# A two-layer transformer kernel in float32: the keys' root rows of the second mixer spread over 128 partitions by a DMA from SBUF to SBUF instead of a product with a row of ones

## The reference, cut to what matters

```python
def mla_mixer(z, cos, sin, qa_g, kva_g, w_uq, w_ukv, qn_g, kn_g):
    cq, ckv, kpe = jnp.split(z, [MLA_Q_LORA, MLA_Q_LORA + MLA_KV_LORA], axis=-1)
    q = (rms_norm(cq, qa_g) @ w_uq).reshape(B, S, MLA_HEADS, MLA_QK)
    kv = (rms_norm(ckv, kva_g) @ w_ukv).reshape(B, S, MLA_HEADS, MLA_NOPE + MLA_VDIM)
    k_nope, v = kv[..., :MLA_NOPE], kv[..., MLA_NOPE:]
    k_rope = jnp.broadcast_to(kpe[:, :, None, :], (B, S, MLA_HEADS, MLA_ROPE))
    k = jnp.concatenate([k_nope, k_rope], axis=-1)
    q = rms_norm(q, qn_g)
    k = rms_norm(k, kn_g)
    q = jnp.concatenate([q[..., :MLA_NOPE], apply_rope(q[..., MLA_NOPE:], cos, sin)], axis=-1)
    k = jnp.concatenate([k[..., :MLA_NOPE], apply_rope(k[..., MLA_NOPE:], cos, sin)], axis=-1)
    o = causal_block_attention(q, k, v)
    return o.reshape(B, S, MLA_HEADS * MLA_VDIM)
```

## Time and profile before

| | us |
|---|---|
| median of 3 runs | 1857.9 (1856.42 to 1859.65) |
| the profiled execution | 1856.39 |
| its span | 1854.6 |
| PE busy | 1807.7 (97%) |
| DVE busy | 931.0 |
| ACT busy | 729.7 |
| POOL busy | 708.0 |

### The profile page before, as it was taken

The page is one execution under the profiler, slowest core; times in us unless marked ns, Lnnn a source line. Parts: engine busy times, 40 slices in busy tenths (PEclk is TensorE's granted clock), DMA queues, the critical chain, the costliest instruction groups (busy, mean ns, idle before and its releaser), DMA issues.

```text
span 1854.6 us, 24525 instructions
## 1 busy us (share of the span) xinstructions
PE 1807.7 (97%) x9589; PEld 1471.0 (79%) x9589; DVE 931.0 (50%) x1290; ACT 729.7 (39%) x960; POOL 708.0 (38%) x221
## 2 busy tenths in 40 slices
PE   7989999999999999999999999999999999999998
PEld 5789866888888887666888888888887788888886
DVE  4365874556553116565455565235427734413564
ACT  4143143455554224554355555322214542221423
POOL 1253812344434443231343443444234333343332
PEclk9999999999999999999999999999999999999999
DMA  7632101322232232120223222323321122323221
GB/s 285 257 114 92 47 24 46 114 90 90 93 104 78 93 107 89 36 69 24 69 97 107 90 90 89 104 95 121 80 91 46 47 79 85 122 92 101 81 69 68
DMA packets 28185, 170.33 MB, mean 92 GB/s; under 512 B 3024, under 2 KB 5328, under 8 KB 11728
## 3 DMA queue, kind: packets, MB, share of 16 engines
q1 hardware_dynamic: 24720, 151.20, 23.9%
q10 hardware_dynamic: 3392, 18.09, 2.9%
HBM read 167.18 MB, written 2.10 MB: 91 GB/s over the span
## 4 chain that ended last, share of the span: by engine, by line
PE 72%; issue 16%; DVE 4%; POOL 4%; ACT 2%; DMA 0%; POOLq 0%; ACTq 0%; DVEq 0%
PE ps L393 43%; PE ps L808 12%; POOL wlo L1182 4%; PE ps L664 1%; PE ps L1073 1%; PE ps L1056 1%; PE ps L533 1%; PE ps L534 1%; PE ps L535 1%; PE ps L1085 1%; PE ps L1083 1%; PE ps L1084 1%; PE ps L899 1%; PE ps L413 1%; PE ps L415 1%
## 5 line engine op out<-in xcount | busy, mean ns | idle before, releaser
L1182 POOL TENSOR_TENSOR wlo<-wraw,whi 128x2048 fp32r<-128x2048 f32 (+3 forms) x148 | 626.8, 4236 | 1025.7 <-ACT whi L1296 1007.7
L393 PE MATMUL ps<-hh,whi 128*128 128x512 f32 x1344 | 528.2, 393 | 1.3 <-POOL wlo L1182 0.7
L393 PE MATMUL ps<-hh,wlo 128*128 128x512 f32 x1344 | 523.7, 390 | 0.0
L393 PE MATMUL ps<-hl,whi 128*128 128x512 f32 x1344 | 523.6, 390 | 0.0
L1296 ACT ACTIVATE whi<-wraw 128x2048 fp32r<-128x2048 f32 (+3 forms) x149 | 265.2, 1780 | 364.8 <-PE ps L393 292.2
L393 PEld LDWEIGHTS ps<-hh,whi 128*128 128x128 f32 x1344 | 252.4, 188 | 57.2 <-issue 3.2
L393 PEld LDWEIGHTS ps<-hl,whi 128*128 128x128 f32 x1344 | 252.5, 188 | 52.5 <-issue 1.2
L393 PEld LDWEIGHTS ps<-hh,wlo 128*128 128x128 f32 x1344 | 252.4, 188 | 52.6
L2144 DVE SCALAR_TENSOR_TENSOR scr<-ps,vec,scr 128x510 f32<-128x510 f32 (+1 forms) x176 | 120.2, 744 | 93.1 <-ACT scr L1500 93.1
L808 PE MATMUL ps<-gh,whi 128*128 128x512 f32 x352 | 137.8, 391 | 1.3 <-DVE gl L2159 1.3
L808 PE MATMUL ps<-gh,wlo 128*128 128x512 f32 x352 | 137.1, 390 | 0.0
(11 more groups left out here) (461 smaller groups left out, 2808.4 us busy)
## 6 DMA issues: line engine op xcount, KB each, us to landing
wraw<-in_w SPq DMA_DIRECT2D x63, 1024.0 KB, 4.9
wraw<-in_w0b SPq DMA_DIRECT2D x26, 1024.0 KB, 4.9
wraw<-in_w1o SPq DMA_DIRECT2D x26, 1024.0 KB, 4.9
wraw<-in_wd SPq DMA_DIRECT2D x32, 704.0 KB, 4.0
ada<-in_wada ACTq DMA_DIRECT2D x12, 1024.0 KB, 8.1
xtok<-in_x SPq DMA_DIRECT2D x4, 512.0 KB, 8.6
out<-ytok SPq DMA_DIRECT2D x4, 512.0 KB, 4.0
wraw<-in_w SPq DMA_DIRECT2D x3, 576.0 KB, 3.8
```

Source lines behind the costliest of these rows:

```text
L393: last = mm(o, l, r, start=(k == 0 and n == 0), stop=(k == K - 1 and n == 2))
L1182: nc.gpsimd.tensor_tensor(wlo[:, s % 2, 0:wd], wraw[:, s % 2, 0:wd], whi[:, s % 2, 0:wd].bitcast(F32), ALU.subtract).then_inc(lo_ready, 1)
```

## The change

Jobs 10 and 11 disappear from PE. `BANKED` is the list of jobs without them, and the two banks now go round in that list. In their place SP issues two DMAs per pair, each of which reads one row of `rstd4` (partition 64 or 96, 512 float32, 2 KB) 128 times and writes it to the 128 partitions of `krow[0]` or `krow[1]` (256 KB each). They wait for `m_rs` of the pair, from the second pair on also until DVE has taken the rows of the pair before. They stand in SP's order behind the load of slot `S_UQ + 3`, of slot `S_UQ + 5`, and of slot `S_O1 + 1`, and ahead of the next one. ACT's Ln of pairs 1 and 2 waits until the DMAs of the pair before have read `rstd4`. DVE waits for both DMAs of the pair (`krow_in`) ahead of job 10 and reads the row from SBUF.

```diff
+    krow = [w("krow0", 76, [P, T]), w("krow1", 80, [P, T])]
...
+        krow_in = sem("krow_in")
...
         FLAT = sum(JOBS, ())
+        BANKED = tuple(j for j in FLAT if j[1] < 10)
         def place(pr, k):
-            return FLAT.index((pr, k))
+            return BANKED.index((pr, k))
         def taken(pr, k):
-            return sum(j not in (5, 6, 8) for _, j in FLAT[:place(pr, k) + 1])
+            return sum(j not in (5, 6, 8) for _, j in FLAT[:FLAT.index((pr, k)) + 1])
         def finished(pr, k):
-            return sum(j not in (2, 6) for _, j in FLAT[:place(pr, k) + 1])
+            return sum(j not in (2, 6) for _, j in BANKED[:place(pr, k) + 1])
...
             load_many(S_Z1, 4, dr["w1"])
+            def key_rows(pr):
+                sp.wait_ge(m_rs, pr + 1)
+                if pr:
+                    sp.wait_ge(m_ev, taken(pr - 1, 11))
+                for e in range(2):
+                    row = rstd4[64 + 32 * e:65 + 32 * e, :].unsqueeze(1).to_broadcast([1, P, T])
+                    sp.dma_start(krow[e][:], row).then_inc(krow_in, 16)
+
             for j in range(6):
                 load(S_UQ + j, dr["w1"][4 + j][:, 0:(1152, 1024)[j % 2]])
-            load_many(S_O1, 26, dr["w1o"])
+                if j in (3, 5):
+                    key_rows(j // 2 - 1)
+            load(S_O1, dr["w1o"][0])
+            load(S_O1 + 1, dr["w1o"][1])
+            key_rows(2)
+            load_many(S_O1 + 2, 24, dr["w1o"][2:26])
...
             def job(pr, k):
+                if k >= 10:
+                    return
                 i = place(pr, k)
...
                 else:
-                    bp, bk = FLAT[i - 2]
+                    bp, bk = BANKED[i - 2]
...
-                else:
-                    g = k - 8
-                    last = mm(ps[:, bank, :], con[32 * g:32 * g + 1, COFF["ones"]:COFF["ones"] + P], rstd4[32 * g:32 * g + 1, :],
-                              start=True, stop=True)
...
                 elif k == 8:
                     act.wait_ge(m_mm, finished(pr, k))
+                    if pr:
+                        act.wait_ge(krow_in, 32 * pr)
                     link(A(rstd4, ps[:, FB + place(pr, k) % 2, :], ACT.Ln, bias=cc("qke"), scale=cc("qks")))
...
             def job(pr, k):
-                b = ps[:, FB + place(pr, k) % 2, :]
                 if k in (5, 6, 8):
                     return
-                if k == 2:
+                b = krow[k - 10][:] if k >= 10 else ps[:, FB + place(pr, k) % 2, :]
+                if k >= 10:
+                    dve.wait_ge(krow_in, 32 * pr + 32)
+                elif k == 2:
                     dve.wait_ge(used, S_UQ + 2 * pr + 1)
```

## The result

| | before | after |
|---|---|---|
| median, us | 1858.77 (1856.42 to 1859.65, 4 runs) | 1896.3 (1894.74 to 1897.89, 4 runs) |
| profiled execution's span, us | 1854.6 | 1892.9 |
| PE busy, us | 1807.7 | 1806.9 |

The ratio after to before is 1.0209, with a 95% interval of 1.0194 to 1.0223: the change makes the kernel 36 to 41 us slower. The span grew by 38.3 us. The forecast was 1897.0 us for the profiled execution, which took 1894.74 us (before: 1856.39).

The account below looks back on a forecast made before the run. PE, busy 1807.7 of 1854.6 us, was taken to bound the kernel. Stalls 41.6 less 5.8 given back plus 4.8 for the clock made 40.6 us on 1856.4: 1897.0 us, range 1853 to 1910.

Parts of the forecast that it names:

- The price of a DMA: Row DMAs on the queue: 9.5 us for 256 KB, 21.3 us for a pair including 2.3 us fixed time.
- The mechanism: Row DMAs: sixteen engines take turns at the one source partition, so all go at one engine's pace, 27.6 GB/s.
- The stalls: DVE ahead of job 10 in the three pairs: stands still 12.0, 15.5 and 14.1 us, together 41.6 us.
- Given back: DVE's former idling for PE behind pairs 0 and 1 disappears: 5.8 us, the removed products' 4.2 us inside it.
- the clock: Granted clock on PE falls behind each of three stalls: 1.6 us of lost work each, 4.8 us in all.
- the operand in SBUF: DVE's twelve products with the root row read it from SBUF instead of PSUM: nothing taken for that.
- The loads: Weight loads moved behind the row DMAs, such as slots S_UQ + 4 and S_O1: cost nothing more beside the stall.
- What is removed: Six products with ones on PE, 1.05 us each: four in pairs 0 and 1 worth 4.2 us, pair 2's nothing.
- rival A: Row DMAs land in time, PE's 4.2 us come off: 1852.2 to 1854.4 us; chance 0.25 including a no-effect case.

Follow-up runs that it names:

- adj16: Changed kernel, each row DMA reading 16 neighbouring partitions with the same root, 8 times each, instead of one partition 128 times; one run, 1854.75 us.
- step16: Changed kernel, each row DMA reading 16 partitions, every second of the 32 with the same root, 8 times each; one run, 1855.8 us.
- unused_rows: Kernel before, products kept, plus the six row DMAs in the change's places and ACT's wait for them; nobody reads the rows; median 1870.71 us, ratio 1.0070.
- free_row: Changed kernel without row DMAs or products with ones; DVE multiplies by the sine table already in SBUF (wrong scaling); median 1857.76 us, ratio to before 0.9998.
- sbuf_operand: Kernel before with all its products, but DVE reads the second operand of jobs 10 and 11 from SBUF (sine table, wrong scaling); ratio 1.0006.
- mixed: early_row0, but pair 2 keeps its two products with ones on PE and has no row DMAs; median 1855.71 us, ratio to before 0.9992.
- early_row0: wide32 with job 11 of pair 0 one step earlier on DVE, right behind job 10; median 1855.61 us, ratio to before 0.9987.
- wide32: Changed kernel, each row DMA reading all 32 partitions with the same root, 4 times each, instead of one; median 1857.16 us, ratio to before 1.0002.

## Why the prediction was right, and where it was not

**The price of a DMA** held: 9.5 us for 256 KB was forecast and 9.0 us measured between the two landings, 21.3 us for a pair and 20.85 us from issue to DVE's start (794.56 - 773.71). The mechanism, that a single source partition lets the engines take turns, was an argument by a destination of sixteen partitions; adj16 against step16 shows it, with groups of neighbours in place of single partitions. Nothing in the rows of before could tell these two apart.

**The stalls** were forecast at 12.0, 15.5 and 14.1 us and were 11.52, 14.87 and 13.50, all ahead of job 10 and none ahead of job 11, as forecast.

**Given back and the clock** came out right only in their sum, and that is luck. For the pieces behind each Exp, the net loss less the stall is +1.1, -4.2 and +1.6 us; forecast were +0.3 (1.6 of clock less 1.26), -3.0 (1.6 less 4.55) and +1.6. The clock cost more than forecast: with PE at work it stood at 0.50 or below full from about 797.6 to 804 us, some 2.7 us of lost work, and by the same count some 2.3 and 1.5 us behind the other two stalls, 6.5 us in all against 4.8. The terms that hide it are estimates, what is left when the clock is taken off. Behind pair 0 two DVE operations of job 11 met GpSimd and took 3.4 us more, while the 1.1 us that the normalisation had lost to GpSimd before were not lost there now. I had taken nothing for the operand in SBUF; this term was missing, and some 3.8 us given back, instead of 1.26, cover it. Behind pair 1 some 6.5 us were given back instead of 4.55. In sum the net was -1.5 us where the forecast had -1.0. On the profiled executions the forecast was 40.6 us and the difference 38.35: 1.7 us of the gap are the stalls (39.9 in place of 41.6), 0.5 us the rest. That the medians lie closer to 1897 is chance.

**The loads** cost nothing beside the stall, as forecast; unused_rows shows that by themselves, with the clock that falls behind them, they cost 10 us behind pair 0 and 14 us in the mixer.

**What is removed** was wrong. I counted four products at 4.2 us for rival A. free_row, with nothing in their place, gained nothing that could be measured, and its mixer was 1.9 us longer. The forecast did not rest on it, since the term was inside what is given back, but A's time of 1852 to 1854 did not exist: with rows in time the time is that of before. Pair 1's two products were worth 2.7 us (2.1 forecast), pair 0's cost 2.8 us, or 0.8 us with job 11 moved out of GpSimd's way, and pair 2's were worth nothing, as forecast. The step that failed is that a product on the chain is worth its own length: DVE and GpSimd move against each other when PE's part shortens. What the remaining 0.8 us behind pair 0 is stays open.

## What to carry to other kernels

Before a row is spread over partitions by a DMA inside SBUF, ask from how many partitions it is read, and how far these lie apart: one partition gave 29 GB/s to all sixteen engines together, eight neighbours 50, sixteen neighbours 109, sixteen spread over 32 partitions 187. Here the same root stood in 32 partitions already, and reading all of them took the slowest DMA from 20.2 to 4.4 us with one line. With a source of eight partitions only half of the DMA engines were busy. And the product that is taken off the chain's busiest engine is worth its length only if the others' order still fits: measure it with a kernel in which the replacement is free before building the replacement.

## What was not expected of the hardware

- DVE's product with all operands in SBUF took 3.13 us beside a GpSimd operation and 0.75 us without; a normalisation with one operand, also in SBUF, took 1.76 us beside one and 0.62 us without; an operation with an operand in PSUM took 0.69 us beside the same GpSimd operation. That moving an operand from PSUM to SBUF can cost 2.4 us where the two meet follows from comparing these different operations; no run changes the place alone, and where they do not meet (sbuf_operand) it cost nothing.
- The granted clock fell to 0.50 in steps where PE idled for only a few us in short pieces. mixed had the same two pieces of idle time there as before (0.20 and 1.00 us), and early_row0 nearly the same as wide32 and adj16 (1.40 and 2.21 us); the clock fell in mixed and early_row0 and not in the others. What decides it is not in these rows.
